# Turning raw exponentials with transposes and dividing the attention rows after the value products

## The reference

```
s = einsum('bqhd,bnhd->bqhn', q, k) * HEAD_DIM ** -0.5     # 16 heads, 4 KV heads, HEAD_DIM 64
s = where(selected, s, -inf)
p = softmax(s, axis=-1)
o = einsum('bqhn,bnhd->bqhd', p, v)                        # then  out = o @ w_o
```

## Time and profile before

| | |
|---|---|
| median of 3 runs | 2173.11 us (2162.26 to 2175.85) |
| the profiled execution | 2166.78 us, its span 2164.9 us |
| PE busy | 1982.6 us, 92% of the span |
| DVE, ACT, POOL busy | 856.4, 597.8, 513.2 us |
| granted clock, mean of the span | 0.947 |
| blocks of the prompt's attention | 615 to 786 us of the span |
| decode attention | to 821 us |

### The profile page before, as it was taken

How to read it: one execution, slowest core, us unless ns; L and a number is a source line. 1 busy time by engine, 2 the same in 40 slices (tenths; PEclk the granted TensorE clock), 3 DMA queues, 4 the chain that set the end, 5 groups by cost and what they waited for, 6 DMA issues and landing times.

```text
span 2164.9 us, 36160 instructions
## 1 busy us (share of the span) xinstructions
PE 1982.6 (92%) x15485; PEld 1899.4 (88%) x15485; DVE 856.4 (40%) x1163; ACT 597.8 (28%) x837; POOL 513.2 (24%) x438
## 2 busy tenths in 40 slices
PE   5999999999887668999999999999997389999996
PEld 5999999988864448899999989999997379999995
DVE  2433322447737512633332243333224653333223
ACT  2221221442233332522121252122113452212123
POOL 2211111342200263411111231111121741111120
PEclk9999999999768889999999999999999689999998
DMA  5453222261100122233322223323221222332321
GB/s 170 136 170 97 82 88 94 82 146 40 43 0 1 33 86 79 65 91 97 90 84 96 82 78 97 96 79 96 88 93 35 59 75 81 97 97 81 104 69 40
DMA packets 258366, 179.55 MB, mean 83 GB/s; under 512 B 10806, under 2 KB 254782, under 8 KB 257757
## 3 DMA queue, kind: packets, MB, share of 16 engines
q1 hardware_dynamic: 250000, 154.90, 24.5%
q10 hardware_dynamic: 6165, 10.79, 1.8%
q0 software_dynamic: 2112, 12.59, 1.7%
HBM read 169.57 MB, written 8.08 MB: 82 GB/s over the span
## 4 chain that ended last, share of the span: by engine, by line
PE 80%; issue 7%; DVE 5%; POOL 3%; ACT 3%; DMA 1%; POOLq 0%; ACTq 0%; DVEq 0%
PE ps L798 71%; PE ps L897 2%; PE ps L841 2%; PE ps L902 1%; PE ps L1000 1%; DVE xf L1249 1%; ACT w_hi L512 1%; DVE xf L1255 1%; DVE w_lo L1223 1%; PE ps L982 1%; POOL diag L1812 1%; PE ps L882 1%; POOL sum_sq L1736 1%; ACT xf L548 1%; POOL sum_z L1734 1%
## 5 line engine op out<-in xcount | busy, mean ns | idle before, releaser
L798 PE MATMUL ps<-xh,w_hi 128*128 128x260 f32 x3040 | 640.4, 287 | 39.4 <-ACT xh L543 17.7
L798 PE MATMUL ps<-xh,w_lo 128*128 128x260 f32 x3040 | 633.8, 284 | 0.0
L1223 DVE TENSOR_TENSOR w_lo<-w_raw,w_hi 128x2048 fp32r<-128x2048 f32 (+2 forms) x153 | 444.9, 2909 | 407.9 <-ACT w_hi L512 407.9
L798 PEld LDWEIGHTS ps<-xh,w_hi 128*128 128x128 f32 x3040 | 486.7, 191 | 45.2 <-issue 25.9
L798 PEld LDWEIGHTS ps<-xh,w_lo 128*128 128x128 f32 x3040 | 487.8, 191 | 0.2
L798 PE MATMUL ps<-xl,w_hi 128*128 128x260 f32 x3040 | 383.6, 283 | 1.3 <-POOL xl L1840 1.3
L798 PEld LDWEIGHTS ps<-xl,w_hi 128*128 128x128 f32 x3040 | 372.6, 189 | 1.6 <-POOL xl L1840 1.5
L512 ACT CAST w_hi<-w_raw 128x2048 fp32r<-128x2048 f32 (+2 forms) x153 | 281.9, 1843 | 282.5 <-PE ps L798 262.9
L798 PE MATMUL ps<-hh,w_hi 128*128 128x260 f32 x1408 | 292.9, 283 | 0.0
L798 PE MATMUL ps<-hh,w_lo 128*128 128x260 f32 x1408 | 291.4, 282 | 0.0
L1666 DVE TENSOR_TENSOR hid<-silu_g,ps 128x520 f32<-128x520 f32 x88 | 61.2, 696 | 548.8 <-ACT silu_g L711 514.7
(11 more groups left out here) (250 smaller groups left out, 1555.0 us busy)
## 6 DMA issues: line engine op xcount, KB each, us to landing
w_raw<-in_ffn_wi_dram SPq DMA_DIRECT2D x176, 512.0 KB
w_raw<-in_ffn_wo_dram SPq DMA_DIRECT2D x32, 1024.0 KB
w_raw<-in_ffn_wo_dram SPq DMA_DIRECT2D x16, 768.0 KB
w_raw<-in_attn_w_in_dram SPq DMA_DIRECT2D x8, 1024.0 KB
keys_scratch<-key_half POOLq DMA_DIRECT2D x2, 2048.0 KB, 8.0
w_raw<-in_attn_w_o_dram SPq DMA_DIRECT2D x4, 1024.0 KB
x_in<-in_x_prompt_dram ACTq DMA_DIRECT2D x1, 2048.0 KB
out_dram<-y_out ACTq DMA_DIRECT2D x4, 512.0 KB
```

The source lines that it names most:

```text
L798: mm = nc.tensor.matmul(ps[0:mc, bank + 2 * m + h, 0:HT], w[:, k, m, 0:mc], x(k)[:, h * HT:(h + 1) * HT], start=first and k == 0 and w is ...
L1223: nc.vector.tensor_tensor(w_lo[:, c % 2, 0:n], w_raw[:, c % 2, 0:n], w_hi[:, c % 2, 0:n].bitcast(F32), ALU.subtract).then_inc(s_lo, 1)
```

## The change

`probs` turns the raw exponentials by a plain transpose against the identity, so it waits for the exponentials (`s_exp`) and no longer for `diag` (`s_p`), and POOL makes no `diag` at all. `values` swaps its operands: the turned exponentials (128 columns) are stationary and 64 value columns move, with one product per head and key tile, so the result has queries on partitions. A new DVE step `divide` multiplies it by the inverse row sums into `o_tok`, and a new PE step `turn` transposes that twice back into the layout that `out_high` and `out_low` read, now PSUM columns 256 to 511. POOL starts the 16 gathers of key rows as soon as the list of rows is there.

```diff
@@ ACT, out_high @@
-                act.wait_ge(s_pv, B + 1)
+                act.wait_ge(s_ot, B + 1)
                 nc.scalar.activation(xh[:, 2 * g:2 * g + 2, i * P:(i + 1) * P],
-                                     ps[:, 4 + B % 2, 0:256].rearrange("p (u q) -> p u q", u=2), ACT.Copy).then_inc(s_oh, 1)
+                                     ps[:, 4 + B % 2, 256:512].rearrange("p (u q) -> p u q", u=2), ACT.Copy).then_inc(s_oh, 1)
@@ PE, probs @@
-                    pe.wait_ge(s_p, B + 1)
+                    pe.wait_ge(s_exp, B + 1)
...
-                            mm = nc.tensor.matmul(ps[:, 2 + t % 2, r * P:(r + 1) * P], sc[:, B % 2, r, j * P:(j + 1) * P],
-                                                  diag[:, B % 2, r, :], start=True, stop=True)
+                            mm = nc.tensor.transpose(ps[:, 2 + t % 2, r * P:(r + 1) * P], sc[:, B % 2, r, j * P:(j + 1) * P], ident)
@@ PE, values @@
-                    for e in range(2):
+                    for r in range(4):
                         for j in range(i + 1):
-                            mm = nc.tensor.matmul(ps[64 * e:64 * e + 64, 4 + B % 2, 0:256],
-                                                  kv_tok[:, j, 256 + g * 64:320 + g * 64],
-                                                  p_t[:, B % 2, j].rearrange("p (u e) q -> p u e q", e=2)[:, :, e, :],
-                                                  start=j == 0, stop=j == i)
-                        if e == 1:
-                            mm.then_inc(s_pv, 1)
-                            side_step()
+                            mm = nc.tensor.matmul(ps[:, 4 + B % 2, r * HEAD_DIM:(r + 1) * HEAD_DIM], p_t[:, B % 2, j, r, :],
+                                                  kv_tok[:, j, 256 + g * 64:320 + g * 64], start=j == 0, stop=j == i)
+                    mm.then_inc(s_pv, 1)
+                    side_step()
+
+                def turn(B):
+
+                    pe.wait_ge(s_o, B + 1)
+                    for u in range(2):
+                        mm = nc.tensor.transpose(ps[:, 4 + B % 2, 256 + u * P:256 + (u + 1) * P],
+                                                 o_tok[:, B % 2, 2 * u:2 * u + 2, :].rearrange("p e d -> p (e d)"), ident)
+                    mm.then_inc(s_ot, 1)
@@ PE, the loop @@
+                    if B >= 2:
+                        turn(B - 2)
                     if B >= 1:
                         values(B - 1, now)
                     probs(B, now)
+                turn(len(BLOCKS) - 2)
                 values(len(BLOCKS) - 1, none)
...
                 sel_transposes(0)
+                turn(len(BLOCKS) - 1)
@@ DVE, the loop @@
                     if B >= 1:
                         inverse(B - 1)
+                    if B >= 2:
+                        divide(B - 2)
 
                     if 2 <= B <= SIDE_BLOCKS + 2:
...
             def inverse(B):
                 dve.wait_ge(s_exp, B + 1)
+                if B >= 2:
+                    dve.wait_ge(s_o, B - 1)
                 nc.vector.reciprocal(row_inv[:, B % 2, :], row_sum[:, B % 2, :]).then_inc(s_rinv, 1)
+
+            def divide(B):
+
+                dve.wait_ge(s_pv, B + 1)
+                dve.wait_ge(s_rinv, B + 1)
+                if B >= 2:
+                    dve.wait_ge(s_ot, B - 1)
+                nc.vector.tensor_tensor(o_tok[:, B % 2], ps[:, 4 + B % 2, 0:256].rearrange("p (r d) -> p r d", r=4),
+                                        row_inv[:, B % 2, :].unsqueeze(2).broadcast_to([P, 4, HEAD_DIM]), ALU.mult).then_inc(s_o, 1)
@@ POOL, attention @@
-                for B, (i, g) in enumerate(BLOCKS):
-                    pool.wait_ge(s_rinv, B + 1)
...
-                    nc.gpsimd.tensor_tensor(diag[:, B % 2], ident.unsqueeze(1).broadcast_to([P, 4, P]),
-                                            row_inv[:, B % 2, :].unsqueeze(2).broadcast_to([P, 4, P]), ALU.mult).then_inc(s_p, 1)
...
+                pool.wait_ge(s_idxl, 16)
+                pool.wait_ge(s_newkv, 32)
+                for _ in range(2 * DEC):
+                    gather()
                 pool.wait_ge(s_s, 4 * len(BLOCKS))
                 nc.gpsimd.memset(q_pad[:], 0.0)
                 nc.gpsimd.memset(p_pad[:], 0.0).then_inc(s_zero, 1)
```

More of the change, by code:

```diff
@@ L181, in trunk_kernel @@
         p_t = at("p_t", [P, 2, NQT, 4, P], offset=h_off)
-        diag = at("diag", [P, 2, 4, P], offset=w_off + 28672)
+        o_tok = at("o_tok", [P, 2, 4, HEAD_DIM], offset=w_off + 28672)
         q_pad = at("q_pad", [P, 2, 1152], offset=h_off + 4 * TOK * 16)
@@ L333, in trunk_kernel @@
         s_rinv = sem("s_rinv")
-        s_p = sem("s_p")
+        s_o = sem("s_o")
+        s_ot = sem("s_ot")
         s_tp = sem("s_tp")
@@ L398, in trunk_kernel @@
         POOL_ORDER = (6, 7, 0, 1, 2, 3, 4, 5)
-        GATHERS = 9
         SIDE_BLOCKS = 7
@@ L1538, in attention @@
                 inverse(len(BLOCKS) - 1)
-                for B in range(len(BLOCKS) - 3, len(BLOCKS)):
+                divide(len(BLOCKS) - 2)
+                out_low(len(BLOCKS) - 3)
+                divide(len(BLOCKS) - 1)
+                for B in range(len(BLOCKS) - 2, len(BLOCKS)):
                     out_low(B)
@@ L1589, in out_low @@
                 nc.vector.tensor_tensor(xl[:, 2 * g:2 * g + 2, i * P:(i + 1) * P],
-                                        ps[:, 4 + B % 2, 0:256].rearrange("p (u q) -> p u q", u=2),
+                                        ps[:, 4 + B % 2, 256:512].rearrange("p (u q) -> p u q", u=2),
                                         xh[:, 2 * g:2 * g + 2, i * P:(i + 1) * P].bitcast(F32), ALU.subtract).then_inc(s_ol, 1)
@@ L1804, in gather @@
                                                  bounds_check=N_PHYS * PAGE - 1, oob_is_err=False).then_inc(s, 16)
-                for B, (i, g) in enumerate(BLOCKS):
-                    pool.wait_ge(s_rinv, B + 1)
-                    if B == 0:
-                        pool.wait_ge(s_madd, NQT)
-                    if B >= 2:
-                        pool.wait_ge(s_tp, tile_base[B - 1])
-                    nc.gpsimd.tensor_tensor(diag[:, B % 2], ident.unsqueeze(1).broadcast_to([P, 4, P]),
-                                            row_inv[:, B % 2, :].unsqueeze(2).broadcast_to([P, 4, P]), ALU.mult).then_inc(s_p, 1)
-                    if B == GATHERS:
-                        pool.wait_ge(s_idxl, 16)
-                        pool.wait_ge(s_newkv, 32)
-                    if B >= GATHERS:
-                        for _ in range(5):
-                            if len(gathers) > 2 * DEC:
-                                gather()
+                pool.wait_ge(s_idxl, 16)
+                pool.wait_ge(s_newkv, 32)
+                for _ in range(2 * DEC):
+                    gather()
                 pool.wait_ge(s_s, 4 * len(BLOCKS))
```

## The result

The changed kernel takes **2221.41 us** (median of 4, 2217.43 to 2224.54) against 2173.2 us (2162.26 to 2175.85) of the kernel before: ratio **1.0228, 95% interval 1.0206 to 1.025**. The forecast was 2214, within 2168 to 2230. The profiled execution has a span of 2221.6 us against 2164.9, and its own time is 2224.54 us, where that of before was 2166.78. So the two traces differ by 56.7 us where the medians differ by 48.2; what follows from traces is compared with the 56.7.

What follows compares the result with a forecast made beforehand. Bound: DVE's stream in turns with side steps, POOL after the list of rows. Full clock 19.6 - 3 - 15 = +1.5, half 55 - 3 - 1 = +51; half in four fifths gives +41: 2214 us, range 2168 to 2230.

Steps and rivals of the forecast that it cites:

- The wait: Turns with side steps: divide waits for the value products ahead of DVE's side steps, making a chain of values, divide, side step.
- The side turns: Attention turns with side steps, before T (list of rows written): +19.6 us at full clock, +55 at half.
- the half-clock sum: Side turns at half clock: 45 us for the added wait, 8 to 9 for scores, 2 for side products, together +55.
- the reserve said there: PE's turning work: some 18 us go but lie under DVE's side steps, a reserve if PE became the bound.
- The neighbour: DVE's first side step without POOL's diag beside it: 0.44 us back in 7 turns, -3 us.
- Which clock: PE clock in the attention: half clock in four fifths, giving +41 between +1.5 at full and +51 at half.
- The tail: After the list of rows: earlier gathers give -15 us at full clock; at half POOL waits for PE, only -1.
- the third rival: Half clock in side turns, full in the tail: +37, 2210 us; chance 0.50 together with the forecast case.
- T + 53: Tail at full clock: products on the gathered values start 53 us after the list of rows, against 67.8 before.
- The clock holds: Rival: PE stays at full clock, value products cost 0.21 us each, 2175 us by the median; chance 0.22.
- Half clock throughout: Rival: every side turn pays and POOL waits for PE in the tail, +51, 2224 us; chance 0.25.
- The wait that costs nothing: Rival: value products end before DVE finishes its maxima, so nothing is late, -18, 2155 us; chance 0.03.

Runs made afterwards that it cites:

- the 0.9996: Kernel before with the products against diag replaced by transposes against the identity, rows not divided by their sums: 2166.12 us, 0.9996.
- `diag` off GpSimd: Kernel before with diag made by ScalarE (first nine blocks) and VectorE (the rest), four value gathers ahead of the clearing: 2158.88 us, 0.9946.
- GpSimd free: Kernel before with the identity in place of diag, key gathers started once the list is there, no division by row sums: 2147.44 us, 0.9914.
- the late divide: Changed kernel with divide moved behind the three side steps: 2175.89 us, 1.0042 of the kernel before.
- the passed waits: Changed kernel with a wait on a long-passed semaphore ahead of every fifth key gather: 2196.94 us, 1.0148 of the kernel before.
- products for transposes: Changed kernel with the probabilities turned by products with the identity instead of transposes: 2180.44 us, 1.0062 of the kernel before.
- shifted code: Changed kernel with 112 passed waits added to each of VectorE's and ScalarE's instructions in an earlier stage: 2222.06 us, 1.0223 of the kernel before.
- more gathers ahead: Changed kernel with divide behind the side steps, products instead of transposes, and six value gathers ahead of the wait for the last scores: 2182.39 us, 1.0051.
- groups of five: Changed kernel with key gathers let go in fives, each group after a further block's row sums: 2197.09 us, 1.0136 of the kernel before.
- the 22 in groups: Changed kernel with divide behind the side steps, products instead of transposes, and 22 gathers ahead of the last scores in fives with waits: 2154.53 us, 0.9955.
- both edits: Changed kernel with divide behind the side steps and products against the identity instead of transposes: 2157.4 us, 0.9952 of the kernel before.

## Why the prediction was right, and what in it was not

**The wait.** Shown. `divide` waits for the value products in every turn, with the side steps behind it. Moving it saved 20.4 us before T.

**The side turns.** By the prediction's terms T had to move by +16.6 at full clock and +52 at half; measured +45.6. That four fifths of the way between is +45 is luck: the clock was not a mixture there, but 0.63, 0.56 and then 0.50 from turn to turn, so the half-clock sum is the one to compare, and it is some 6 us too large. From the first scores of each turn in the two traces, the four turns with four key tiles grew by 5.3, 7.8, 8.5 and 7.7 us, where the terms give about 8 each, and those with three, the last of them up to T, by 6.2, 5.1, 3.8 and 2.9, where they give about 5.5; 1.7 us had been won before. So the terms fit the full turns and are too large for the first and for the last two. The products were mis-sized a little: 6.93 / 16 = 0.43 us each at half clock instead of 0.39, and 0.23 at full (12 in 2.79) instead of 0.21. The turn with its 14.8 us from the scores to the side product is the half-clock turn (15). That the transposes for `diag` were worth nothing there, as costed, fits the 0.9996, with the reserve said there.

**The neighbour.** Shown. The first side step takes 2.38 us (661.99 to 664.37) instead of 2.82, and the difference lies in one small instruction. Here it is in the kernel before, beside `diag` (650.84 to 651.88), and in the kernel with `diag` off GpSimd:

```profile
651.27 0.65 DVE L1452 TENSOR_SCALAR reach<-reach 128x24 f32<-128x24 f32 x1
651.45 0.18 DVE L1462 TENSOR_SCALAR reach<-reach 128x24 f32<-128x24 f32 x1
```

With GpSimd free it takes 0.18 us as well, in all side steps up to 700 us. A clearing does the same on a larger scale: 1.74 us for the four-column `neg_max` in the changed kernel (831.07 to 832.81, the clearing 830.77 to 832.79), and the 4.58 us above. The Trainium skill ("SBUF — State Buffer", SBUF: two separate sides) says that VectorE in a two-port mode, or with two inputs in SBUF beside a GpSimd instruction that reads there, shares a pair of ports with GpSimd as an exclusive lock, and that whoever comes second fully blocks. The trace agrees in this: the steps end 0.04, 0.02 and 0.03 us after GpSimd's instruction. Whether these steps ran in such a mode no trace here shows, and the step of 4.58 us began 0.56 us before the first clearing, while GpSimd issued a gather, which the lock by itself does not explain.

**Which clock.** The forecast took mostly half, and it was 0.63 in the first turn with side products, 0.56 in the next and 0.50 from there on. The reason was half right. Of the two things named, transposes and short value products, neither does it alone: transposes with the old value products gave 0.84, the new value products without transposes 0.90 and 0.73, both 0.55 and 0.50; and with both but the late divide 0.50 and 0.54, so it wasn't the wait. The Trainium skill's rule ("TensorE: Matmul & The Clock Gate", Part 4: PE-mode transpose), that the full clock doesn't engage for transposes, is borne out in that they draw the clock down here, and not as a rule by itself: 784 to 800 ran at 1.00 among transposes, and 575 to 625 stayed at 0.50 without any.

**The tail: here a step failed.** "Of the 15 only -1 is left" at half clock. It failed on the clock of the tail, which the forecast took to be that of the side turns. The kernel with the passed waits reached T + 53.0, the whole -15, although its side turns are at half clock: the clock rose again for the narrow blocks (0.82 over 760 to 820), so the third rival (half in the side turns, full in the tail: +37, 2210) names what happened, but for the stall. The changed kernel has the stall on top, 28.1 us at the start of the products. By the traces, from kernel to kernel: +45.6 - 14.8 + 28.1 - 2.0 = 56.9. The forecast had no term for the stall. That its +41 came near the measured +48 is in good part luck: it gave up most of a gain that was there and so covered part of a loss that it didn't know. Two small errors in its T + 53 cancel as well: the first key gather starts at T + 5.8, not 5.3, and sixteen value gathers take 20.6 us by its own rows (787.26 to 807.83), not 20.9.

**The rivals.** "The clock holds" is the kernel with products for transposes, near enough: forecast +1.5, measured +13 (1.0062), with a clock of 0.90 and 0.73, and T + 58.0. Half clock throughout (+51, 2224) would have given the right number by a tail that was not what ran. The wait that costs nothing is ruled out by the 6.35 us that VectorE stood before the divide.

**What stays open.** Why PE's increments came late. What the traces hold of it: in the eleven kernels without a stall, each of PE's 932 increments between 735 and 880 us is recorded within 0.1 us of the end of its product; in the three with it (the changed kernel, shifted code, more gathers ahead) those of the long stalls come 5 to 16 us late. Of the 256 increments of each of the two gathers' semaphores the traces hold 54 to 57 in these three kernels and 249 to 257 (with a last reset) in the other eleven. That points at the way of the increments while gathers run, and no run here goes further.

A row of gathers with no wait between them is needed: three kernels lost the stall by waits alone (groups of five, the 22 in groups, passed waits). It isn't enough: the late divide, products for transposes, GpSimd free and both edits (16 gathers each) and `diag` off GpSimd (20) have such rows and no stall, and so has every kernel, that before too, in its value gathers. Nor must the wait stand in the row itself: groups of five and passed waits have it in the key gathers only, and the late increments during the value gathers went too.

In the three kernels that have the stall, the value products just ahead of the long one ran at half clock (8 products in 3.51 or 3.52 us); with both edits, with groups of five and with the passed waits the same products ran at full clock (1.90). The half clock came after the first late increments, not before: in the changed kernel the first one (0.5 us late, at 797.71) belongs to 8 value products in 1.90 us, and PE then stood 4.05 us before 802.53. So the low clock did not start it; whether it lengthens it was not told apart.

## What to carry to other kernels

Before an instruction that waits for another engine is put into a queue, look at what stands behind it: here a 0.42 us divide ahead of three side steps cost 20 us, and behind them it cost none of this. Less PE work can mean a lower clock, and then the work that stays pays: the changed kernel did some 18 us less turning and lost 19 to 22 by it. When waits are taken out of a long row of indirect gathers, look in the trace for waits of other engines with no named releaser, and try a passed wait between the gathers if they show; here it took them away three times out of three.

The best complete versions here are `diag` off GpSimd (0.9946), both edits (0.9952) and both edits with grouped gathers (0.9955); their intervals overlap. The 0.9914 of the kernel with GpSimd free lacks the division.

## What the runs showed that I had not expected

- While sixteen or 22 indirect gathers start in a row, 1.30 us apart, PE's semaphore increments can come 5 to 16 us late. VectorE and ScalarE stood for 7 to 17 us on products that had ended, in two kernels until 2.3 us after the last gather, in the third VectorE until just before it and ScalarE until 3.1 us after it. Waits that are already passed, ahead of every fifth gather, removed it at no cost (0.30 us between gathers with and without).
- Two GpSimd clearings of 128 x 2304 in a row (2.0 us each) stretched a four-column VectorE step from 0.17 to 4.58 us, one of them to 1.74 us; a `diag` of 1.04 us stretched a 24-column step from 0.18 to 0.65 us.
- A stretch with PE busy all of 50 us with products stayed at 0.50 of its clock.
